# One layer of a hybrid mixer and expert network: state-space jobs brought forward, attention moved back, and the order of their branches exchanged

## The chip, the cores and the metric

The kernel runs on one core of one Trainium2 chip. The metric is the device time of one execution in microseconds (us). TensorE (PE) multiplies matrices; its results land in PSUM, eight banks of 128 x 512 numbers. VectorE (DVE) and ScalarE (ACT) read them from there. GpSimd (POOL) computes from the on-chip memory SBUF, and SyncE (SP) issues the transfers. Each engine executes its own list of instructions strictly in order, and the lists are tied together by semaphores only.

## What is computed

512 latent tokens and 256 context tokens of width 1024 go through one layer: a modulated norm, one input projection, four mixers side by side, a gated sum of the four, an output projection, and a mixture of 32 experts.

```python
q, k, v, z, xbc, dtr, fu, su = _split_in(h @ w_in)
att = _window_attention(q, k, v, kc, vc, sink)           # 8 heads, window 128, plus all context keys
y, _, _ = _ssm_bidir(xs, bm, cm, dt, a_log, fin_f, fin_b, True)
ssm = _ssm_out(y, xs, z, d_skip, ssm_norm_w)             # state-space mixer, both directions, chunks of 128
branches = jnp.stack([att, ssm, _fourier(fu), _short_conv(su, sconv_w)], axis=2)
gates = jax.nn.sigmoid(h @ w_gate + b_gate).reshape(b, l, N_BRANCHES, d)
proj = jnp.einsum("blnw,nwd->blnd", branches, w_branch)
out = jnp.sum(gates * proj, axis=2) @ w_o
```

Branch 0 is attention, 1 the state-space mixer, 2 the Fourier mixer, 3 the short convolution.

## The kernel before

`timeline()` (line 63) writes out one list of steps, and every engine walks through the same list and emits its part of each step. So the order of that list is the order on every engine. The stretch that matters is the merge. For each branch n in `MIX_ORDER` and each of 8 column tiles d it has ("gate", n, d), 24 matmuls whose result ScalarE turns into `gth` (a tanh), and ("proj", n, d), 4 matmuls of the branch (the branch tile); VectorE multiplies the two and, from the second branch on, adds the product into `merged`. Before each gate ScalarE and VectorE split a weight tile into a high and a low part (`ring_hi`, `ring_lo`).

Behind every gate and every proj stand two calls of `side()` (line 114), the points. A point may put in one step of attention or one state job:

- `attention()`: step h puts in, for even h, O(h/2-2), T(h-2) and S(h/2), and for odd h only T(h-2). S(p) computes the scores of a pair of heads p into banks 3 and 4, with four or five blocks of 128 keys; a fifth block goes to bank 2 for the first head and bank 6 for the second (job "S5"). VectorE scales, masks and takes the maximum of each head, ScalarE takes the exp (`sc`), VectorE normalises (at the T job with the odd number before it), T transposes the probabilities on TensorE into banks 5 and 6, ScalarE copies them (`PT`), O multiplies by the values into bank 2. 16 pairs, the middle eight (4 to 11) with five blocks.
- state jobs: `st` (10 of them, each after an `xdd` that GpSimd makes only when the st before it is done), then for each of 4 chunks and 2 groups G, seg, seg, yoff, y; then ynorm, three empty places and four ytr. G goes to `Gm` on VectorE; seg multiplies `Am` from GpSimd and ScalarE takes its exp into `E`, which VectorE multiplies by `Gm`; yoff and y are read by VectorE into `ytmp`.

`bank_plan()` (line 180) gives each step its bank. `claim` (line 501) makes TensorE wait, ahead of a step's first matmul, until the step that had the bank before has been read. All state jobs but ytr are on bank 7, except that G, y and one seg of chunks 2 and 3 are on banks 3 and 5. A T with an odd number also waits until the next pair's S5 is read:

```python
        elif k in ("G", "y") and s[1] >= 2:
            b = 3
        elif k == "seg" and s[1] >= 2 and s[3]:
            b = 5
```

```python
                if h % 2 and ("S5", (h + 1) // 2) in plan:
                    job_read(pe, ("S5", (h + 1) // 2))
```

The order of branches is 3, 2, 0, 1. Attention stands at every odd point from the first on and a state job at every even one, so that attention ends with the second branch, and the state jobs of chunks 2 and 3 run in the third. After the merge come the output projection ("wo"), whose input `mhi`, `mlo` is written in the last branch, the reload of x into `H` (issued when the last proj is done), the routing, and a loop over the experts, whose weights stream from HBM. GpSimd zeroes `xr` behind the last product of the merge (line 1827) and scatters it to the rows that are never used.

Of the kernel before, what the change touches and what calls it, by code (L numbers as in the profile page):

```python
# [19 lines left out]
FR = mybir.dt.float32r  # L20
# [6 lines left out]
P = 128  # L27
D, KD = 1024, 8
S, NCH = 512, 4
# [4 lines left out]
NE, NG, EPG = 32, 8, 4  # L34
# [22 lines left out]
R_DTB, R_ALOG, R_D, R_SINK, R_RB, R_IE, R_IG, R_IB, R_IH = 0, 16, 32, 40, 48, 80, 112, 120, 248  # L57
R_N = 376

MIX_ORDER = (3, 2, 0, 1)  # L60


def timeline():

    t = [("mr", 0), ("mr", 1), ("ssq",), ("mr", 2), ("ssqc",), ("mr", 3), ("mod", 0)]
    t += [("v",), ("vc",), ("dt",)]
    macc = 0

    def tile(*jobs):


        nonlocal t, macc
        t += [*jobs, ("macc", macc)]
        if macc > 4 and macc % 4 == 1:
            t += [("mod", macc // 4)]
        macc += 1

    for m in range(6):
        tile(("xbc", m), ("xbcc", m))
    tile(("k",), ("kc",))  # L80
    for m in range(4):
        tile(("fu", m), *([("rot", 0)] if m == 0 else []))
    t += [("dec",)]
    for m in range(4):
        tile(("q", m), *([("rot", m)] if m else []))
    for m in range(4):
        tile(("cg", m), *([("rot", 4)] if m == 0 else []))
        tile(("sx", m))
        tile(("bg", m))
    for i in range(4):  # L90
        tile(("zk", i))
    t += [("macc", 31)] + [("z", c) for c in range(NCH)]
    t += [("xtr", c) for c in (4, 5, 0, 1, 2, 3)] + [("btr", 0), ("btr", 1), ("mod", 8)]

    att_step = 0

    def attention():

        nonlocal att_step
        h, att_step = att_step, att_step + 1  # L100
        even = h % 2 == 0
        return ([("O", h // 2 - 2)] * (even and h >= 4) + [("T", h - 2)] * (2 <= h < 34) + [("S", h // 2)] * (even and h < 32))

    t += [("V", 0), ("V", 1), ("F", 0)] + attention() + [("V", 2), ("F", 1)] + attention()
    t += [("V", 3), ("F", 2)] + attention() + [("F", 3)] + attention()

    ssm = [("st", d, k) for k in range(5) for d in range(2)]
    for c in range(NCH):
        for g in range(2):
            ssm += [("G", c, g), ("seg", c, g, 0), ("seg", c, g, 1), ("yoff", c, g), ("y", c, g)]  # L110
    ssm += [("ynorm",)] + [None] * 3 + [("ytr", c) for c in range(NCH)]
    point = 0

    def side():

        nonlocal point
        point += 1
        if point % 2 == 1 and att_step < 35:
            return attention()
        if ssm and (point % 2 == 0 or point % 4 == 3 or len(ssm) < 5):  # L120
            return [x for x in [ssm.pop(0)] if x]
        return []

    for i, n in enumerate(MIX_ORDER):
        if i == 3:
            t += [x for x in ssm if x]
            ssm = []
        for d in range(8):
            t += [("gate", n, d)] + side() + side() + [("proj", n, d)] + side() + side()
    for d in range(8):  # L130
        t += [("wo", d)] + ([("sw",)] if d == 1 else []) + ([("rtk", d - 2)] if d > 1 else [])
    t += [("rtk", 6), ("ssq2",), ("rtk", 7), ("rt",)] + [("h2tr", c) for c in range(NCH)] + [("cnt",), ("bexp",), ("tab",)]
    return t
# [20 lines left out]
def tile_order():  # L154

    steps, order, first, last = timeline(), [], {}, {}
    for i, s in enumerate(steps):
        x = tile_of(s)
        if x is not None:
            if x not in last:  # L160
                order.append(x)
                first[x] = i
            last[x] = s


    cut = [x for x in order if is_split(x)]
    need = dict(first)
    for i, x in enumerate(cut):
        need[x] = first[cut[i - 2]] - 0.5 if i > 1 else 0
    soonest = len(steps)  # L170
    for x in reversed(order):
        if x[0] != "macc":
            soonest = need[x] = min(need[x], soonest)
    return sorted(order, key=lambda x: need[x]), last
# [5 lines left out]
def bank_plan(steps):  # L180


    used, plan, rot = {}, {}, 0
    for s in steps:
        k = s[0]
        if k in ROT3:
            b = rot % 3
            rot += 1
        elif k in ("gate", "proj", "O"):
            b = ("gate", "proj", "O").index(k)  # L190
        elif k == "S":
            b = 3
        elif k == "sw":
            b = 5
        elif k == "h2tr":
            b = 3 + s[1] % 2 * 2
        elif k in ("V", "T"):
            b = 5
        elif k in ("xtr", "btr", "F", "ytr"):
            b = 3 + s[1] % 2 * 4  # L200
        elif k in ("G", "y") and s[1] >= 2:
            b = 3
        elif k == "seg" and s[1] >= 2 and s[3]:
            b = 5
        elif k == "ssq2" or s == ("mod", 0):
            b = 0
        elif k == "ssqc":
            b = 1
        elif k == "ssq":
            b = 3  # L210
        elif k in ("ynorm", "macc", "zk", "rtk", "dt"):
            continue
        elif k == "mr":
            b = 4 + s[1]
        elif k == "z":
            b = 3 + s[1]
        elif k == "rt":
            b = 7
        elif k == "cnt":
            b = 2  # L220
        elif k == "tab":
            b = 2
        else:
            b = 7
        used[b] = used.get(b, 0) + 1
        plan[s] = (b, used[b])
        if k == "S" and len(head(2 * s[1])[3]) > 4:
            used[2] = used.get(2, 0) + 1
            plan["S5", s[1]] = (2, used[2])
    return plan  # L230


def head(h):


    blk, g, j = h // 8, h % 2, h // 2 % 4
    if blk == 0:
        return blk, g, j, [0, 1, 4, 5], 3 * P
    keys = [4, 5] + [c for c in (blk - 1, blk, blk + 1) if c < NCH]
    return blk, g, j, keys, 0  # L240
# [33 lines left out]
def build(nc, xT, ctxT, adaw, stream, consts, cossin, dft, cols, rows, wv, wrt, umap, wa, wb, w2, h2d, ybuf, outT):  # L274
# [3 lines left out]
    def at(name, off, shape, dt=F32):  # L278
        return nc.alloc_sbuf_tensor_at(name, shape, dt, offset=BASE + off)
# [11 lines left out]
    hcx = at("hcx", 157888, [P, KD, SC])  # L291
    hchi = at("hchi", 118976, [P, KD, SC], FR)
    hclo = at("hclo", 49152, [P, KD, SC], FR)
    mhi = at("mhi", 110784, [P, KD, S], FR)
    mlo = at("mlo", 49152, [P, KD, S], FR)
    dftm = at("dftm", 49152, [P, 2, NCH, S])
    merged = at("merged", 49152, [P, KD, S])
# [19 lines left out]
    qT = at("qT", 127168, [P, 4, S])  # L317
    dts = at("dts", 127168, [P, 8, 96])
    WV = at("WV", 130240, [P, KD, VD])
    ssmT = at("ssmT", 127168, [P, 4, S])  # L320
    kT = at("kT", 135360, [P, S])
    kcT = at("kcT", 137408, [P, SC])
    vt = at("vt", 138432, [P, 6, P])
# [10 lines left out]
    def up(n):  # L334
        return (n + 31) // 32 * 32
# [25 lines left out]
    m0 = SLOTS * 3 * UNIT * 4  # L361
# [1 line left out]
    um = at("um", m0, [P, UM_N]); m0 += up(UM_N * 4)  # L363
    ru = at("ru", m0, [P, 2]); m0 += 32
    vrow = at("vrow", m0, [P, 2, NTAB]); m0 += up(2 * NTAB * 4)
    swk = at("swk", m0, [P, KD, NE]); g16 = at("g16", m0, [P, 4, NCH, 16]); m0 += 1024
    swv = at("swv", m0, [P, NE]); m0 += 128
    rst = at("rst", m0, [P, 2, NCH]); m0 += 32
    lg = at("lg", m0, [P, NCH, NE]); m0 += 512
    both = at("both", m0, [P, 2, NCH, NE]); sel = at("sel", m0, [P, NCH, NE]); m0 += 512  # L370
# [36 lines left out]
    def bk(b, n=1):  # L407

        return psum[:, b:b + n, :].rearrange("p b n -> p (b n)")

    steps = timeline()
    plan = bank_plan(steps)
    full = [ctx.enter_context(nc.semaphore(f"bank_full{i}")) for i in range(8)]
    empty = [ctx.enter_context(nc.semaphore(f"bank_read{i}")) for i in range(8)]

    def sem(name):
        return ctx.enter_context(nc.semaphore(name))
# [18 lines left out]
    gate_done, merge_done = sem("gate_done"), sem("merge_done")  # L436
# [55 lines left out]
    def job_full(eng, s):  # L492
        b, n = plan[s]
        eng.wait_ge(full[b], n)

    def job_read(eng, s):

        b, n = plan[s]
        eng.wait_ge(empty[b], n)
# [17 lines left out]
    def _(sp):  # L517
# [11 lines left out]
        for i, x in enumerate(order):  # L529
# [12 lines left out]
            if x == ("wo", 2):  # L542

                job_full(sp, ("gate", MIX_ORDER[-1], 7))
                job_full(sp, ("proj", MIX_ORDER[-1], 7))
                sp.dma_start(WR[:, :, :], wrt).then_inc(wr_in, 16)
# [469 lines left out]
    def _(act):  # L1016
        t = Tally(act)
        def A(out, in_, f, **kw):
            return nc.scalar.activation(out, in_, f, **kw)  # L1019
# [20 lines left out]
        for s in steps:  # L1040
# [142 lines left out]
            elif k0 == "gate":  # L1183
                n, d = s[1:]
                b, _n = plan[s]
                job_full(act, s)
                i = MIX_ORDER.index(n) * 8 + d
                if i:

                    job_read(act, ("proj", MIX_ORDER[(i - 1) // 8], (i - 1) % 8))  # L1190
                else:
                    job_read(act, ("z", 3))
                    act.wait_ge(half_ready, 1)
                A(gth[:, :], bk(b), ACT.Tanh, scale=0.5, bias=half[:, n * 8 + d:n * 8 + d + 1]).then_inc(*t(empty[b], plan[s][1]))
            elif k0 == "proj" and s[1] == MIX_ORDER[-1]:

# [590 lines left out]
    def _(g_):  # L1787
        t = Tally(g_)
        G_ = nc.gpsimd

        def hb(ap, n):
            return ap.unsqueeze(2).to_broadcast([P, ap.shape[1], n])

        seg_i = 0
        for s in steps:
            k0 = s[0]
            t.settle()
            if k0 == "st":
                d, k = s[1:]
# [10 lines left out]
            elif k0 == "seg":  # L1810
# [10 lines left out]
                if g == 0:  # L1821
                    if c:
# [1 line left out]
                    G_.tensor_tensor(xd[:, d, :].rearrange("p (h n) -> p h n", h=8),  # L1824
                                     xs[:, c, :].rearrange("p (h n) -> p h n", h=8),
                                     hb(dtv[:, c, d * 8:d * 8 + 8], HD), ALU.mult).then_inc(*t(xd_ready))
        g_.wait_ge(merge_done, 32)
        for h in range(2):
            G_.memset(xr[h][:, :], 0.0).then_inc(*t(xr_zero))
        t.settle()  # L1830
# [196 lines left out]
```

## Time and profile before

| | |
|---|---|
| median of three runs | 1328.28 us (1327.74 to 1329.34) |
| the profiled execution | 1328.5 us |
| its span, first to last instruction | 1326.7 us |
| TensorE busy | 1183.2 us, 89% |
| VectorE busy | 520.0 us, 39% |
| ScalarE busy | 303.5 us, 23% |
| GpSimd busy | 127.2 us, 10% |
| mean DMA rate over the span | 207 GB/s |

The span divides by what goes on: norms and modulation to some 50 us, the input projection to some 285, transposes and the Fourier mixer to 336, the merge with its attention steps and state jobs to 738, the output projection to some 798, the routing to some 831, the experts to some 1280, the final norm to the end. In a timeline row the first number is the start within the span and the second the length; a matmul's end is modelled, so the start of the next instruction is the better mark of how long TensorE needs. In brackets stands the idle time of the engine ahead of the row and what ended it. "L600", "L1286" and "L1019" are lines of helpers, so that operations are told apart by their tiles.

### The profile page before, as it was taken

Reading aid. Unit: us, or ns where it says so; the run is one execution under the profiler, and the core shown is the slowest. Engines: PE = TensorE matmul, PEld = TensorE weight load, DVE = VectorE, ACT = ScalarE, POOL = GpSimd, SP = SyncE. Lnnn points to the kernel's source line nnn. Section 1 sums busy time; section 2 is a strip of 40 time slices with the busy share of each in tenths; the row PEclk is TensorE's granted clock in tenths of the full one; section 3 lists DMA queues with packets and bytes.
Section 4 is the critical chain, followed back from the end, with each engine's and each line's share of the span. In section 5 each row is a group of like instructions: output and inputs, shape, how many; then the busy total and the mean of one; then the engine's idle time right before and its main releaser. Section 6 shows DMA issues by size and latency. Waiting matters only on the chain.

```text
span 1326.7 us, 15684 instructions
## 1 busy us (share of the span) xinstructions
PE 1183.2 (89%) x5560; PEld 699.7 (53%) x5560; DVE 520.0 (39%) x914; ACT 303.5 (23%) x514; POOL 127.2 (10%) x182
## 2 busy tenths in 40 slices
PE   6799999989999999999999895599999997777844
PEld 1588878864666666666666684233333332222212
DVE  2776457632576676544433336011110100001016
ACT  2633122231333334212322233011111110000002
POOL 0000000000111010111000100122121121111110
PEclk9899799989999999999999896799999999999987
DMA  9234535430011111112122301999999999999942
GB/s 390 80 131 149 197 127 214 170 109 0 30 67 65 48 49 48 49 48 82 62 96 95 136 16 71 405 408 423 425 418 420 429 417 425 427 425 426 425 171 105
DMA packets 40019, 274.50 MB, mean 207 GB/s; under 512 B 7428, under 2 KB 7940, under 8 KB 28064
## 3 DMA queue, kind: packets, MB, share of 16 engines
q1 hardware_dynamic: 34208, 265.41, 49.7%
q0 software_dynamic: 5760, 8.41, 1.7%
q8 instruction: 32, 0.52, 0.2%
q14 instruction: 19, 0.16, 0.0%
HBM read 270.90 MB, written 13.37 MB: 214 GB/s over the span
## 4 chain that ended last, share of the span: by engine, by line
PE 73%; DMA 15%; DVE 7%; ACT 2%; issue 1%; SPq 0%; DVEq 0%; ACTq 0%; POOLq 0%; POOL 0%
PE psum L600 70%; DMA ering<-in_wb 11%; DMA Hx<-in_xT 1%; PE psum L824 1%; PE psum L929 1%; DVE amx L1499 1%; DMA gat<-expert_rows 1%; DVE sc L1488 1%; DMA xr<-token_rows,tabt 1%; DMA H<-in_xT 1%; PE psum L949 1%; PE psum L1007 0%; DVE ytmp L1286 0%; ACT E L1019 0%; ACT Hx L1019 0%
## 5 line engine op out<-in xcount | busy, mean ns | idle before, releaser
L600 PE MATMUL psum<-ering,xs 128*64 128x512 f32 x1056 | 242.1, 608 | 41.0 <-DMA ering<-in_wb 22.4
L600 PE MATMUL psum<-Hhi,ring_hi 128*128 128x512 f32 x472 | 195.9, 415 | 1.0 <-ACT gth L1019 1.0
L600 PE MATMUL psum<-Hlo,ring_hi 128*128 128x512 f32 x472 | 186.7, 396 | 0.0
L600 PE MATMUL psum<-Hhi,ring_lo 128*128 128x512 f32 x472 | 185.4, 393 | 0.0
L1286 DVE TENSOR_TENSOR sg<-sg,psum 128x256 f32<-128x256 f32 x66 | 27.8, 421 | 380.9 <-ACT sg L1019 379.7
L600 PEld LDWEIGHTS psum<-ering,xs 128*64 128x64 f32 x1056 | 73.3, 139 | 187.2 <-issue 132.8
L600 PE MATMUL psum<-ering,at 128*64 128x512 f32 x528 | 119.5, 597 | 0.8 <-ACT at L1019 0.8
L1286 DVE TENSOR_TENSOR ring_lo<-ring,ring_hi 128x1024 fp32r<-128x1024 f32 x71 | 87.7, 1235 | 51.6 <-ACT ring_hi L1019 50.2
L600 PEld LDWEIGHTS psum<-Hhi,ring_hi 128*128 128x128 f32 x472 | 89.7, 190 | 27.5 <-issue 9.0
L600 PEld LDWEIGHTS psum<-Hlo,ring_hi 128*128 128x128 f32 x472 | 89.8, 190 | 21.8 <-issue 4.3
L600 PEld LDWEIGHTS psum<-Hhi,ring_lo 128*128 128x128 f32 x472 | 89.6, 190 | 20.2
L1019 ACT ACTIVATE ring_hi<-ring 128x1024 fp32r<-128x1024 f32 x71 | 75.3, 1060 | 90.5 <-PE psum L600 49.2
L1019 ACT ACTIVATE sg<-psum 128x256 f32<-128x256 f32 x33 | 12.7, 384 | 277.6 <-PE psum L600 277.6
L600 PEld LDWEIGHTS psum<-ering,at 128*64 128x64 f32 x528 | 35.5, 136 | 65.0 <-issue 65.0
L1807 POOL TENSOR_TENSOR xdd<-xs,wdd 128x512 f32<-128x512 f32 x10 | 10.4, 1043 | 392.4 <-DVE zs L1475 285.6
L1019 ACT ACTIVATE ysb<-psum 128x512 f32<-128x512 f32 x33 | 19.7, 597 | 123.2 <-PE psum L600 118.7
L1019 ACT ACTIVATE gth<-psum,half 128x512 f32<-128x512 f32 x32 | 22.0, 688 | 108.3 <-PE psum L600 108.3
L1837 POOL DMA_INDIRECT xr<-token_rows,idx x35 | 37.0, 1056 | 30.6 <-POOL idx L1843 30.6
L1019 ACT ACTIVATE sc<-sc,amx 128x512 f32<-128x512 f32 (+1 forms) x32 | 24.8, 775 | 60.4 <-DVE amx L1500 60.4
L600 PE MATMUL psum<-ada,sil 128*2 128x512 f32 x64 | 29.3, 616 | 9.5 <-DMA ada<-in_adaw 9.5
L1578 DVE SCALAR_TENSOR_TENSOR mtmp<-gth,psum 128x512 f32<-128x512 f32 x24 | 16.5, 687 | 54.5 <-PE psum L600 51.1
L1850 POOL DMA_INDIRECT expert_rows<-ysb,idx x33 | 34.1, 1035 | 28.5 <-POOL idx L1857 28.5
(300 smaller groups left out, 1501.9 us busy)
## 6 DMA issues: line engine op xcount, KB each, us to landing
ering<-in_wa SPq DMA_DIRECT2D x28, 2048.0 KB, 18.3
ering<-in_wb SPq DMA_DIRECT2D x28, 2048.0 KB, 23.0
ering<-in_w SPq DMA_DIRECT2D x28, 2048.0 KB, 26.5
ring<-in_stream SPq DMA_DIRECT2D x87, 512.0 KB, 4.1
ada_ring<-in_stream SPq DMA_DIRECT2D x32, 512.0 KB, 3.3
ada<-in_adaw SPq DMA_DIRECT2D x4, 2048.0 KB, 17.6
gat<-expert_rows SPq DMA_DIRECT2D x4, 1024.0 KB, 8.2
Hx<-in_xT SPq DMA_DIRECT2D x1, 2048.0 KB, 16.6
```

Of the source, the lines that this page charges most:

```text
L600: return nc.tensor.matmul(out, lhsT, rhs, start=start, stop=stop)
L824: ins = nc.tensor.transpose(bk(b, 2)[:, i * P:i * P + P], sc[:, h % 3, i * P:i * P + P], ID)
L929: ins = nc.tensor.transpose(XT[h][:, q * P:q * P + P], xr[h][:, q * P:q * P + P], ID)
L949: ins = nc.tensor.transpose(AT[h][:, q * P:q * P + P], sg[h][:, q * P:q * P + P], ID)
L1019: return nc.scalar.activation(out, in_, f, **kw)
L1286: return V_.tensor_tensor(out, a, b, op)
L1488: ins = V_.scalar_tensor_tensor(sc[:, h % 3, 0:S], bk(3 + g), HD ** -0.5, CT[:, C_MASK + mo:C_MASK + mo + S], ALU.mult, ALU.add)
L1499: link(V_.tensor_reduce(amx[:, h, 0:1], sc[:, h % 3, 0:W], AX.X, ALU.max))
L1578: V_.scalar_tensor_tensor(merged[:, d, :] if first else mtmp[:, :], gth[:, :], 1.0, bk(b), ALU.add, ALU.mult).then_inc(*t(empty[b], plan[s ...
L1807: G_.tensor_tensor(xdd[:, :].rearrange("p (h n) -> p h n", h=8), xs[:, c, :].rearrange("p (h n) -> p h n", h=8), hb(wdd[:, c, d * 8:d * 8 ...
L1837: G_.indirect_dma_start(out=xr[h][:, :], out_offset=None, in_=token_half, in_offset=bass.IndirectOffsetOnAxis(ap=at_rows, axis=0), bounds_ ...
L1850: G_.indirect_dma_start(out=row_half, in_=rows_[:, :], in_offset=None, out_offset=bass.IndirectOffsetOnAxis(ap=idx[:, 2 + h:3 + h], axis=0 ...
```

## The change

The order of branches becomes 3, 2, 1, 0. A point now takes a state job whenever one is left, and behind it, besides, an attention step: up to point 64 (the first two branches) at every fifth point, after that at two of three. State jobs must be done when the third branch begins, attention when the fourth does. The rule that put jobs of chunks 2 and 3 on banks 3 and 5 is gone. `mhi` and `ssmT` change places in SBUF, `swk` and `swv` too, and GpSimd zeroes `xr` only behind the last tile of the output projection, because `mhi` now overlaps that region.

```diff
-MIX_ORDER = (3, 2, 0, 1)
+MIX_ORDER = (3, 2, 1, 0)
...
         nonlocal point
         point += 1
-        if point % 2 == 1 and att_step < 35:
-            return attention()
-        if ssm and (point % 2 == 0 or point % 4 == 3 or len(ssm) < 5):
-            return [x for x in [ssm.pop(0)] if x]
-        return []
+        out = [ssm.pop(0)] if ssm else []
+        if att_step < 35 and (point % 5 == 1 if point <= 64 else point % 3):
+            out += attention()
+        return [x for x in out if x]
 
     for i, n in enumerate(MIX_ORDER):
-        if i == 3:
+        if i == 2:
             t += [x for x in ssm if x]
             ssm = []
+        if i == 3:
+            while att_step < 35:
+                t += attention()
...
         elif k in ("xtr", "btr", "F", "ytr"):
             b = 3 + s[1] % 2 * 4
-        elif k in ("G", "y") and s[1] >= 2:
-            b = 3
-        elif k == "seg" and s[1] >= 2 and s[3]:
-            b = 5
...
-    mhi = at("mhi", 110784, [P, KD, S], FR)
+    mhi = at("mhi", 149696, [P, KD, S], FR)
...
-    ssmT = at("ssmT", 127168, [P, 4, S])
+    ssmT = at("ssmT", 157888, [P, 4, S])
...
-    swk = at("swk", m0, [P, KD, NE]); g16 = at("g16", m0, [P, 4, NCH, 16]); m0 += 1024
-    swv = at("swv", m0, [P, NE]); m0 += 128
+    swk = at("swk", 98304, [P, KD, NE]); g16 = at("g16", m0, [P, 4, NCH, 16]); m0 += 1024
+    swv = at("swv", 99328, [P, NE])
...
-        g_.wait_ge(merge_done, 32)
+        job_full(g_, ("wo", KD - 1))
```

How this moves TensorE's instructions is seen at two places. The first, before the change, is TensorE's list from the last score matmuls of S(9) to G(0,1), around the last branch tile of the first branch. `kT` and `kcT` belong to S, `xd,E` is y(0,0), `scT` the branch tile, `CT,sc` T(17), `xbcT` alone G.

```order
L600 MATMUL psum<-kT,qT 128x128 [waits bank_read5,bank_read2]
L600 MATMUL psum<-kT,qT 128x128
L600 MATMUL psum<-xd,E 128x64 [waits xd_ready,m_ready,bank_read7]
L600 MATMUL psum<-xd,E 128x64 x7
L600 MATMUL psum<-scT,ring 128x512 [waits bank_read1]
L600 MATMUL psum<-scT,ring 128x512 x3
L824 MATMUL psum<-CT,sc 128x128 [waits bank_read2,prob_ready,bank_read5]
L824 MATMUL psum<-CT,sc 128x128 x4
L600 MATMUL psum<-xbcT 128x128 [waits bank_read7]
```

The same two state jobs after the change, on TensorE, now around the branch tile of d = 3. `Am,CT` is the second seg of chunk 0, `prevS,xbcT` its yoff.

```order
L598 MATMUL psum<-Am,CT 128x512 [waits am_ready,bank_read7]
L598 MATMUL psum<-prevS,xbcT 128x256 [waits bank_read7] x2
L598 MATMUL psum<-scT,ring 128x512 [waits bank_read1]
L598 MATMUL psum<-scT,ring 128x512 x3
L598 MATMUL psum<-xd,E 128x64 [waits xd_ready,m_ready,bank_read7]
L598 MATMUL psum<-xd,E 128x64 x7
L598 MATMUL psum<-xbcT 128x128 [waits bank_read7]
```

Between y and G, both on bank 7, stood a branch tile and a T job; now G follows y directly, and yoff follows seg.

The second place is S(9) and T(17) on TensorE after the change, which now stand behind the first branch tile of the third branch.

```order
L822 MATMUL psum<-CT,sc 128x128 [waits prob_ready,bank_read5]
L822 MATMUL psum<-CT,sc 128x128 x4
L598 MATMUL psum<-kcT,qT 128x128 [waits bank_read3]
L598 MATMUL psum<-kcT,qT 128x128 x3
L598 MATMUL psum<-kT,qT 128x128 x4
L598 MATMUL psum<-kT,qT 128x128 [waits bank_read5,bank_read2]
L598 MATMUL psum<-kT,qT 128x128
L822 MATMUL psum<-CT,sc 128x128 [waits bank_read2,prob_ready,bank_read5]
L822 MATMUL psum<-CT,sc 128x128 x4
L598 MATMUL psum<-Hhi,ring_hi 128x512 [waits bank_read0,lo_ready,hi_ready]
```

The wait for bank_read2 at T(17) is the one for S5 of pair 9. In the first fence y(0,0) and the branch tile stood between it and S(9); now nothing does. The same holds for S(11) and T(21).

## Rows read from the trace of the kernel before

**Rows 1.** The page: its head and TensorE's busy time.

```profile
span 1326.7 us, 15684 instructions
...
PE 1183.2 (89%) x5560; PEld 699.7 (53%) x5560; DVE 520.0 (39%) x914; ACT 303.5 (23%) x514; POOL 127.2 (10%) x182
```

**Rows 2.** Table by stretches: window: length, then PE, PEld, DVE, ACT, POOL, PEclk, DMA.

```profile
330.00:552.00 222.00, 217.46 (x1278) 148.94 (x1276) 146.82 (x306) 82.39 (x158) 23.66 (x22) 1.00 0.15 53
552.00:740.00 188.00, 185.34 (x717) 124.57 (x716) 79.63 (x115) 45.28 (x61) 12.40 (x11) 0.99 0.19 68
748.00:757.00 9.00, 6.25 (x29) 5.34 (x28) 3.01 (x4) 4.60 (x6) 0.00 (x0) 0.78 0.44 168
```

**Rows 3.** TensorE's waits by releaser, 330 to 740 us (total, times, longest).

```profile
PE psum L600 <- ACT E L1019: 2.4, 4, 0.9
PE psum L600 <- DVE prevS L1286: 1.8, 3, 1.0
```

**Rows 4.** Timeline at an st job and the gate behind it (start, length, engine).

```profile
362.83 0.65 PE L600 MATMUL psum<-xdd,btm 128*64 128x256 f32 x4
...
363.41 0.50 PE L600 MATMUL psum<-Hhi,ring_hi 128*128 128x512 f32 x1
...
363.62 1.05 POOL L1807 TENSOR_TENSOR xdd<-xs,wdd 128x512 f32<-128x512 f32 x1 [3.61 <-PE psum L600]
...
369.11 1.09 PE L600 MATMUL psum<-PT,vt 128*64 128x128 f32 x16
```

**Rows 5.** Timeline at a yoff job, a branch tile and a y job.

```profile
639.92 1.13 PE L600 MATMUL psum<-prevS,xbcT 64*128 64x256 f32 x4
...
640.98 3.70 PE L600 MATMUL psum<-attT,ring 128*128 128x512 f32 x8
641.15 0.69 DVE L1286 TENSOR_TENSOR ytmp<-psum,dec 128x512 f32<-128x512 f32 x1 [3.58 <-PE psum L600]
644.51 1.89 PE L600 MATMUL psum<-xd,E 128*128 128x64 f32 x16
```

**Rows 6.** Timeline from an S step to the second seg behind it.

```profile
461.84 0.71 PE L600 MATMUL psum<-kcT,qT 64*128 64x128 f32 x8
...
463.26 1.12 PE L600 MATMUL psum<-Am,CT 128*128 128x512 f32 x2
...
464.23 3.60 PE L600 MATMUL psum<-uT,ring 128*128 128x512 f32 x8
...
465.98 0.29 DVE L1495 SCALAR_TENSOR_TENSOR sc<-psum,CT 128x128 f32<-128x128 f32 x1
...
469.26 1.12 PE L600 MATMUL psum<-Am,CT 128*128 128x512 f32 x2 [0.89 <-ACT E L1019]
...
470.47 0.60 ACT L1019 ACTIVATE E<-psum 128x512 f32<-128x512 f32 x1 [0.53 <-PE psum L600]
```

**Rows 7.** Timeline at y(2,0) and the G(2,1) behind it.

```profile
580.43 1.89 PE L600 MATMUL psum<-xd,E 128*128 128x64 f32 x16
...
583.51 0.42 DVE L1286 TENSOR_TENSOR ytmp<-ytmp,psum 128x256 f32<-128x256 f32 x1
...
583.98 0.48 PE L600 MATMUL psum<-xbcT 64*128 64x128 f32 x2 [1.66 <-DVE ytmp L1286]
```

**Rows 8.** Timeline from an S step with four key blocks to yoff.

```profile
507.15 0.71 PE L600 MATMUL psum<-kcT,qT 64*128 64x128 f32 x8
...
508.25 1.13 PE L600 MATMUL psum<-Am,CT 128*128 128x512 f32 x2
...
513.55 1.13 PE L600 MATMUL psum<-prevS,xbcT 64*128 64x256 f32 x4 [0.31 <-ACT E L1019]
```

**Rows 9.** Timeline of GpSimd and of VectorE around the output projection.

```profile
740.34 0.99 POOL L1829 MEMSET xr<- 128x512 f32 x2 [122.41 <-DVE merged L1286]
...
796.93 0.75 DVE L1603 SCALAR_TENSOR_TENSOR H<-psum,A,H 128x512 f32<-128x512 f32 x1 [4.24 <-PE psum L600]
...
831.23 1.03 POOL L1837 DMA_INDIRECT xr<-token_rows,tabt  x1 [84.78 <-DVE tabt L1731]
```

## The prediction

> **What bounds the kernel now.** I first read the page's busy table and the chain that ended last: TensorE is busy for 1183.2 us of a 1326.7 us span [rows 1], and its matmuls make most of the chain. Then the table by stretches. In the part that the change reorders, 330 to 740 us, TensorE is busy 217.46 of 222 us and 185.34 of 188 us [rows 2]: 7.20 us of idle in 410. So the reader should see two things. Nothing but TensorE's own work bounds this part, and since the change removes no matmul, it can win 7.2 us there at most. What it can lose is open: each new wait of TensorE, which executes strictly in the order of the list, goes onto the end. The waits by releaser [rows 3] say what the 7.2 us are: an E tile (exp) still being read on ScalarE, a state result still being read on VectorE; and single waits, the longest of them 1.66 us, which comes up below.
>
> Behind 740 us the work is serial (output projection, routing, experts) and nothing there runs ahead of the last branch, so a shift at 740 us reaches the end one to one.
>
> **The change, part by part.** The matmuls are the same before and after; I price only waits. Prices are start-to-start times of a job and the next one allowed on the same bank, minus the time TensorE needs for the job itself. A gate takes 5.7 us on TensorE (363.41 to 369.11 [rows 4]), a branch tile 3.53 us (640.98 to 644.51 [rows 5]).
>
> Before, one state job stands at a point and then a gate or a branch tile, which hides the reading of bank 7. After, two state jobs follow each other behind every gate and every branch tile. Jobs 1 to 10 are st, then per chunk G, seg, seg, yoff, y twice, so the 58 jobs make 29 pairs. All are on bank 7, because the rule that gave banks 3 and 5 to chunks 2 and 3 is gone too.
>
> *Pairs of st.* Five, one with attention between its halves; four are bare. The second st needs xdd, which GpSimd makes only after the first st: start 362.83, GpSimd 363.62 plus 1.05, so 1.9 us with the handoff, while the st itself takes 0.58 [rows 4]. 4 x 1.4 = 5.5 us.
>
> *Pairs inside a chunk.* Of 20, four (G, seg) have attention between and cost nothing in themselves; 16 are bare:
> - seg, yoff and seg, seg: ScalarE starts the exp 1.21 us after the seg starts and takes 0.60 [rows 6]; next job at 1.86, seg itself 0.97 (463.26 to the branch tile at 464.23). 8 x 0.89 = 7.1 us.
> - yoff, y: VectorE starts reading at 1.23 and takes 0.69 [rows 5], next job at 1.98, own time 1.06: 3 x 0.92. The fourth stands behind a branch tile of branch 2, where VectorE first does the product and the addition of that tile and is late by 0.44: 1.36. Together 4.1 us.
> - y, G: the trace has exactly this pair once, behind a branch tile after the first branch: y starts at 580.43, VectorE first multiplies and adds the tile and prepares its sum, reads the bank at 583.51 for 0.42, and G starts at 583.98 after 1.66 us of idle [rows 7]. One pair is like that: 1.66. One is in the first branch, without the addition (0.6 us shorter): 1.05. Two are behind a gate, where VectorE is free and only the 0.42 us read and the handoff stand: 0.75 each. Together 4.2 us.
>
> Sum 15.4 us.
>
> *A seg behind an attention step.* Its exp is queued on ScalarE behind the two softmax exps. In the trace the S step starts at 461.84 and bank 7 is free at 469.26, 7.42 us later [rows 6]. After the change, S (1.42), seg (0.97) and then a gate (5.7) cover it, but for chunks 1 and 3 only a branch tile (3.53) follows: 7.42 - 5.92 = 1.5 us, twice: 3.0 us.
>
> *The third branch.* Two of three points hold an attention step, so T(2p-1) stands directly behind S(p) four times. For pairs 9 and 11, which have a fifth key block, T waits until VectorE has read the second head's fifth block, 466.27 - 461.84 = 4.43 us after S starts [rows 6]; S itself takes 1.42. 2 x 3.06 = 6.1 us. Pair 13 has four blocks and a gate behind it, which covers everything. Pair 15 has four blocks and only a branch tile before the next O, which waits for T's copy behind the exps: 6.4 us after S starts (507.15 to 513.55, where it was an exp of the same 0.60 [rows 8]). S (1.10), T (some 0.5, an estimate: four of the transposes of which five take 0.7) and the tile cover 5.2: 1.2 us. Sum 7.3 us. VectorE was busy 146.82 of 222 us with one pair per gate and the state jobs beside it [rows 2]; a third more pairs without state jobs I take as no bound yet.
>
> *At no cost.* ynorm now stands before an attention step and a gate, which hide its table loads. The zeroing of xr and its scatters move from the end of the merge to behind the last output projection: GpSimd took 740.34 to 746.45 for them and then idled 84.78 us until 831.23; from about 797 (the last H update) it would be done near 804 [rows 9]. If that cover were gone it would cost up to 6.1 us. The new places of mhi, ssmT, swk and swv move no instruction, and no DMA is added: WR, um and H are still issued behind the last branch tile, whichever branch it is.
>
> **Sum.** Added 5.5 + 15.4 + 3.0 + 7.3 = 31.2; removed: at most the old 7.2, and all of it, since each old wait belongs to a pattern that I have priced anew. Net +24.0. Against the profiled execution's own 1328.5 us that is 1352.5; the median of the runs is 0.2 us lower, which I leave.
>
> The ends: no handoff price could be under zero, so a gain is bounded by -7.2 us. Above, the dearest price seen for a pair (1.66) for all 20 bare pairs gives 33 instead of 21, or +36 in all.
>
> **A rule of the Trainium skill.** The trace shows a granted clock of 1.00 and 0.99 over the stretches with the idles of up to 1.66 us, and 0.78 in the 9 us that hold a 2.75 us wait [rows 2]. That is between the two levels of 1.2 and 2.4 GHz; a fall of this kind in the reordered part is rival 4 below. The Trainium skill, "TensorE: Matmul & The Clock Gate", section "A second HAM failure mode: psum-queue depth-cycling", says that a kernel which cycles through PSUM banks and so pauses briefly and often can make the clock swing between its levels. By that rule the sum would be some 10 us worse; the rows of this case show pauses of the size added here without it, only less often.
>
> **The rivals.**
> 1. *Forecast: the pairs cost their turnaround.* For it: the one such pair in the trace cost 1.66 us as computed. 1347 to 1358 us, likeliest 1352.5. Chance 0.68.
> 2. *VectorE was the hidden limit and moving attention away frees it.* The old waits on prevS and ytmp come from VectorE's queue. If TensorE then found bank 7 read each time, the pairs and the third branch cost nothing and the idle goes: 1328.5 - 7.2 = 1321.3 us, faster. It decides from the point where the mean added wait of the 25 places (20 bare pairs, 2 seg, 3 in the third branch) falls under 0.3 us (7.2 / 25). Against it: the reads themselves take 0.42 to 0.69 us plus handoff. Chance 0.03.
> 3. *Half of it is absorbed*, because waits in a row share one cause, so that the job behind a late one finds its input ready: +12, 1340.5 us. Chance 0.12.
> 4. *The clock falls* under the frequent pauses: at a mean granted 0.95, a quarter of the way from 1.00 to the 0.78 of [rows 2], over the some 200 us of the first two branches, 200 x 0.05 = 10 us more: 1362.5 us. Chance 0.08.
> 5. *VectorE becomes the bound in the third branch*, attention steps queueing there: six steps late by 1.5 us, +9: 1361.5 us. Chance 0.06.
> 6. *It cancels*: within 0.2% of before (2.7 us, about what a measurement of this kernel can tell from no change). Chance 0.03.
>
> **How the numbers follow.** The forecast, rival 1, is the likeliest: 1352.5 us. The range 1340 to 1362 takes in 1, nearly all of 3 and parts of 4 and 5. Faster: rival 2, 0.03. Same: 0.03. Slower: the rest, 0.94.
>
> **What would show it.** In the changed profile TensorE's waits between 330 us and the end of the merge should sum to near 31 us instead of 7. By releaser: xdd on GpSimd or prevS four times about 1.4; E on ScalarE ten times, eight near 0.9 and two near 1.5; ytmp on VectorE eight times from 0.7 to 1.7; and in the third branch two waits near 3 us of T for the VectorE read of sc. H's load, near 740 now, should be issued near 764. The expert stage should keep its length. The clock row over the merge should stay at 1.0. Wrong would be: waits for bank 7 missing in the bare pairs (rival 2), a clock row of 0.9 (rival 4), or waits for VectorE in the third branch at places I have not named (rival 5).

## The result, and the profile after

The changed kernel takes 1364.05 us (median of four runs, 1357.71 to 1366.76) against 1328.01 us before: slower, ratio 1.0264 with a 95% interval of 1.0226 to 1.0303. With five more runs of it, taken later, the nine lie between 1357.71 and 1370.06 us with a median of 1364.42. The forecast of 1352.5 us had the sign, the place and the waits; the time is 12 us further up and 2 us outside the range.

The page of the profiled execution, which is the fastest of the nine (1357.71 us), against [rows 1]: the same 5560 matmul instructions keep TensorE busy for 8.3 us more.

```profile
span 1355.9 us, 15684 instructions
...
PE 1191.5 (88%) x5560; PEld 700.6 (52%) x5560; DVE 516.6 (38%) x914; ACT 303.5 (22%) x514; POOL 128.9 (10%) x182
```

TensorE's waits by releaser in the merge of the changed kernel, 342 to 771.2 us (total, times, longest), against [rows 3]:

```profile
PE psum L598 <- ACT E L1017: 9.1, 10, 1.5
PE psum L598 <- DVE ytmp L1284: 7.6, 8, 1.7
PE psum L822 <- DVE sc L1493: 6.2, 2, 3.1
PE psum L598 <- DVE prevS L1284: 4.0, 2, 2.0
PE psum L598 <- POOL xdd L1805: 3.1, 2, 1.6
PE psum L598 <- ACT PT L1017: 1.3, 1, 1.3
PE psum L598 <- DVE attT L1509: 0.8, 1, 0.8
```

They sum to 32.1 us, where 31.2 were forecast and 7.2 stood before. This is ten waits on E, eight on ytmp, four at st pairs, two of 3.1 us in the third branch: the list of the prediction, entry by entry. One is new, 0.8 us on attT.

The start of the merge is the first matmul of the first gate. Its end is marked by SyncE's issue of WR, which waits for the last branch tile. In the kernel before:

```profile
336.14 0.48 PE L600 MATMUL psum<-Hhi,ring_hi 128*128 128x512 f32 x1
...
738.80 0.33 SPq L546 DMA_DIRECT2D WR<-in_wrt  x1
```

In two profiled executions of the changed kernel, the first and one of the later five (1365.19 us):

```profile
333.18 0.47 PE L598 MATMUL psum<-Hhi,ring_hi 128*128 128x512 f32 x1
...
771.17 0.33 SPq L544 DMA_DIRECT2D WR<-in_wrt  x1
```

```profile
337.30 0.47 PE L598 MATMUL psum<-Hhi,ring_hi 128*128 128x512 f32 x1
...
778.60 0.33 SPq L544 DMA_DIRECT2D WR<-in_wrt  x1
```

The merge ends 32.4 us later in one and 39.8 us later in the other. But it also starts at different times, 3.0 us earlier than before in the first and 1.2 us later in the second, although the change leaves the order of the instructions ahead of it as it was. Its own length is 402.7 us before, 438.0 and 441.3 us after: 35.3 and 38.6 us more. The waits account for 32.1 - 7.2 = 24.9 us in both, since the second execution has the same list of waits to the tenth. What is left is 10.4 and 13.7 us, and it is no wait. The table by stretches of the two executions (window: length, then busy time of PE, PEld, DVE, ACT, POOL, and PEclk, the granted clock as a share of 2.4 GHz), first the one of 1357.71 us, then the one of 1365.19 us:

```profile
342.00:556.00 214.00, 189.46 (x872) 123.80 (x871) 110.95 (x214) 52.14 (x90) 37.24 (x32) 0.96 0.13 45
556.00:600.00 44.00, 44.00 (x234) 31.02 (x234) 23.90 (x44) 15.44 (x25) 0.00 (x0) 1.00 0.21 72
600.00:690.00 90.00, 82.53 (x512) 58.72 (x510) 53.20 (x114) 35.91 (x71) 0.00 (x0) 0.96 0.15 53
690.00:771.20 81.20, 81.20 (x302) 54.95 (x299) 27.04 (x35) 19.18 (x25) 0.00 (x0) 1.00 0.22 78
```

```profile
342.00:556.00 214.00, 190.24 (x861) 124.71 (x860) 106.86 (x205) 50.00 (x86) 38.25 (x33) 0.94 0.13 47
...
600.00:690.00 90.00, 82.52 (x529) 58.74 (x528) 56.85 (x123) 35.69 (x71) 0.00 (x0) 0.96 0.15 53
```

In the first execution the clock is below 1.00 exactly in the two stretches that hold the waits, and 1.00 in the two that hold none. The reader should compare [rows 2], where the same work ran at 1.00 and 0.99. What the clock took can be estimated from these rows, as the missing share times the length: 0.04 x 214 + 0.04 x 90 = 12.2 us in the first, 0.06 x 214 + 0.04 x 90 = 16.4 us in the second, 0.01 x 188 = 1.9 us before. The differences, 10.3 and 14.5 us, are close to the 10.4 and 13.7 us that were left. What a lower clock does to a matmul is seen behind the wait of 1.66 us at G(2,1) in the timeline of the changed kernel (start, length, engine):

```profile
482.20 0.49 PE L598 MATMUL psum<-xbcT 64*128 64x128 f32 x2 [1.66 <-DVE ytmp L1284]
...
483.46 0.42 PE L598 MATMUL psum<-Hlo,ring_hi 128*128 128x512 f32 x1
483.69 0.62 PE L598 MATMUL psum<-Hhi,ring_lo 128*128 128x512 f32 x1
484.11 0.63 PE L598 MATMUL psum<-Hhi,ring_hi 128*128 128x512 f32 x1
484.53 0.63 PE L598 MATMUL psum<-Hlo,ring_hi 128*128 128x512 f32 x1
```

From 483.69 on they start 0.42 to 0.43 us apart instead of 0.23: the lower level, 1.2 GHz. Behind the merge the changed kernel gains 3.2 us back in both executions: 1.7 between the issue of WR and that of the first expert weights, the rest behind it. Over the 87 to 89 us of the first of these stretches the clock was 0.85 in both executions and 0.83 before, which would account for the 1.7; the rest stays open.

### The profile page after: what moved, and what is told of

It is laid out like the page before. It is cut to its first block, busy times and chain, and to the rows that moved or that the text cites. A ratio compares the mean times of both kernels' runs of the same rounds, so it can differ in the third digit from the quotient of the medians.

```text
span 1355.9 us, 15684 instructions
## 1 busy us (share of the span) xinstructions
PE 1191.5 (88%) x5560; PEld 700.6 (52%) x5560; DVE 516.6 (38%) x914; ACT 303.5 (22%) x514; POOL 128.9 (10%) x182
## 4 chain that ended last, share of the span: by engine, by line
PE 47%; DMA 17%; DVE 6%; issue 2%; ACT 1%; SPq 0%; POOL 0%; DVEq 0%; ACTq 0%; POOLq 0%
PE psum L598 44%; DMA ering<-in_wb 14%; PE psum L822 1%; PE psum L927 1%; DMA gat<-expert_rows 1%; DMA xr<-token_rows,tabt 1%; DMA xr<-token_rows,idx 1%; DVE sc L1486 1%; DVE ytmp L1284 1%; DVE amx L1497 1%; DMA H<-in_xT 1%; ACT E L1017 0%; PE psum L947 0%; DVE x L1780 0%; PE psum L1005 0%
## 5 line engine op out<-in xcount | busy, mean ns | idle before, releaser
L598 PE MATMUL psum<-ering,xs 128*64 128x512 f32 x1056 | 245.4, 614 | 38.6 <-DMA ering<-in_wb 21.0
L1284 DVE TENSOR_TENSOR sg<-sg,psum 128x256 f32<-128x256 f32 x66 | 27.8, 421 | 381.5 <-ACT sg L1017 380.4
L1017 ACT ACTIVATE PT<-psum 128x512 f32<-128x512 f32 (+1 forms) x32 | 20.8, 651 | 86.6 <-PE psum L822 74.6
L1835 POOL DMA_INDIRECT xr<-token_rows,idx x35 | 36.9, 1055 | 30.6 <-POOL idx L1841 30.6
```

What stands on the lines that cost most here:

```text
L598: return nc.tensor.matmul(out, lhsT, rhs, start=start, stop=stop)
L1284: return V_.tensor_tensor(out, a, b, op)
L1835: G_.indirect_dma_start(out=xr[h][:, :], out_offset=None, in_=token_half, in_offset=bass.IndirectOffsetOnAxis(ap=at_rows, axis=0), bounds_ ...
```

## The experiments

Two theories stood at the start. **A**: the loss is the waits, 25 us, and beside them a falling clock, which costs a different amount in each execution. **B**: the loss is the waits, and the excess over the forecast sits elsewhere and is fixed. Each kernel is the changed one with the edit shown, unless another is named. The first four experiments ran in one session, in which the kernel before had a median of 1327.58 us; the last four in another, where it had 1326.23 us. For one profiled execution of each, the merge from its first matmul to the issue of WR:

| kernel | length, us | waits, us | length less waits | mean clock |
|---|---|---|---|---|
| before | 402.7 | 7.2 | 395.5 | 1.00 |
| changed, first | 438.0 | 32.1 | 405.9 | 0.97 |
| changed, again | 441.3 | 32.1 | 409.2 | 0.97 |
| two banks | 414.0 | 16.4 | 397.6 | 0.99 |
| old bank rule | 427.6 | 27.0 | 400.6 | 0.98 |
| attention spread | 431.3 | 27.8 | 403.5 | 0.98 |
| fillers | 427.9 | 12.9 | 415.0, with added work | 1.00 |
| two banks, two xdd buffers | 405.7 | 10.6 | 395.1 | 0.99 |
| all together | 392.3 | 0 | 392.3 | 1.00 |
| pairs in the kernel before | 459.9 | 44.1 | 415.8 | 0.94 |

Apart from the fillers, all do the same work in the merge. The column without the waits grows as the clock falls, from 392 to 398 us at 0.99 and above to 416 us at 0.94: that is the clock's part of the loss.

**The changed kernel again.** No edit.

> The changed kernel unchanged, to see how it spreads. Theory A (waits and clock): TensorE's waits in the merge are 32 us in every execution, the time varies with the granted clock: 0.952 goes with 1358 us and 0.946 with 1366 us, about 8 us for 0.006, and a profile at a lower mean clock shows it low for more of the merge, with the same waits. Theory B (waits alone, and the excess over 1352.5 us sits in a stretch behind the merge): a slower execution has the merge as long as the 1357.7 us one and the expert stage longer.

Measured: 1364.42 us (1362.30 to 1370.06, five runs), waits 32.1 us, whole-span clock 0.947 against 0.952. The span is 7.4 us longer than in the first profile (1363.3 against 1355.9). Of this 3.3 us arise in the merge, without a wait being longer, and 4.1 us ahead of it, where TensorE was busy for 5.2 us more with the same instructions and the clock from 285 us to the first gate was 0.86 instead of 0.96. Over the nine runs the time by and large rises as the whole-span clock falls, from 0.952 at 1357.71 us to 0.944 at 1370.06. So theory A's claim holds, but less than half of this difference is the merge's. Theory B's longer expert stage is not there.

**Two banks for state jobs.**

```diff
+        elif k in ("st", "G", "seg", "yoff", "y"):
+            b = 7 if used.get("jobs", 0) % 2 else 3
+            used["jobs"] = used.get("jobs", 0) + 1
```

> State jobs alternate between bank 3 and bank 7, so that the two of a pair never share a bank; order of steps untouched. The 16 bank waits inside the chunks (13.7 us in the changed kernel's trace) and most of the two seg waits (3.0 us) go; st keeps a wait of some 1.6 us four times for xdd. Waits in the merge fall from 32 to some 17 us. Theory A: the time falls by 15 us for the waits and by 3 to 8 us more since the clock stays up, to 1341 to 1346 us. Theory B: it falls by 15 us only, to 1349 us, with the clock as in the changed kernel. Rival that VectorE's queue and not the bank is what is waited for: the waits stay, under other names, and the time stays within 4 us.

Measured: 1337.08 us (1333.34 to 1339.91, six runs), ratio to before 1.0067. The waits left in the merge, by releaser (the rows of the output projection, swk and mlo, left out):

```profile
PE psum L825 <- DVE sc L1496: 6.2, 2, 3.1
PE psum L601 <- POOL xdd L1808: 5.8, 4, 1.6
...
PE psum L601 <- DVE attT L1512: 1.8, 1, 1.8
PE psum L601 <- ACT PT L1020: 1.3, 1, 1.3
PE psum L601 <- ACT E L1020: 1.3, 2, 0.7
```

16.4 us instead of 32.1: every wait on ytmp and most on E are gone; the two st waits on prevS are now waits on xdd, 1.6 instead of 2.0 us. So the bank was what TensorE waited for inside the chunks, not VectorE's queue. But the time fell by 27 us, not by 16. The clock over the first two branches, 0.94 and 0.96 in the changed kernel's two profiles, was 0.99. Theory A had the direction and was too low (15 plus 3 to 8): the clock gave back some 11.

**The old bank rule put back.** The four deleted lines return.

> Only the deleted bank rule is put back: G, y and one seg of chunks 2 and 3 on banks 3 and 5. Of the waits in these chunks those of seg before yoff, seg before seg and yoff before y go (some 5.2 us), y before G stays (both on bank 3). Theory A: 5 us and up to 3 us of clock, 1356 to 1359 us. Theory B: 1359 us. If the deleted rule were what costs most, the time would fall by more than 10 us.

Measured: 1353.62 us (1351.22 to 1361.10, four runs). Waits 27.0 us, so 5.1 less, as priced. The time fell by 10.8 us against the 1364.42 of the same session, twice the waits. It is below what both theories gave; theory A's allowance for the clock (3 us) was again too small. A fall of more than 10 us had been named as the sign that the deleted rule costs most. The fall is just that, but the waits do not bear the reading out: the rule brings back 5.1 of the 24.9 us that were added, and two banks for all state jobs bring back 15.7.

**Attention spread in the third branch.**

```diff
-        if att_step < 35 and (point % 5 == 1 if point <= 64 else point % 3):
+        if att_step < 35 and (point % 5 == 1 if point <= 64 else point < 69 or point % 2):
```

> Only the placing of attention in the third branch is altered: one step behind each gate and each branch tile (two behind the first two), with the odd T ahead of an S instead of right behind it. The two waits of 3.08 us for the fifth block and the one of 1.3 us for the copy go: 7.5 us less, and under theory A 1 to 3 us of clock besides: 1353 to 1357 us. Theory B: 1356.5 us. If VectorE were the bound in that branch, as rival 5 had it, the waits would reappear on sc and the time fall by less than 3 us.

Measured: 1355.93 us (1354.33 to 1357.23, four runs). The two waits of 3.1 us and the one of 1.3 us are gone, but two new ones on PT have come (1.1 and 1.9 us), where O stands directly behind a T. So the waits fell by 4.3, not 7.5 us, and the time by 8.5: inside the range that was expected (1353 to 1357 us), though 7.5 us of it had been expected from the waits and only 1 to 3 from the clock. By its time alone this run would not separate the theories. The clock of the third branch, 0.96 in the changed kernel, was 1.00 over everything behind 556 us. VectorE is no bound in that branch.

**Fillers.** The test that separates the clock from the waits: TensorE multiplies constants where it would wait.

```diff
+        jobs = ("st", "G", "seg", "yoff", "y")
+        fill = {}
+        for i_, s in enumerate(steps):
+            if s[0] in jobs and steps[i_ - 1][0] in jobs:
+                fill[s] = (6, 3 if s[0] == "st" else 1)
+            if s in (("T", 17), ("T", 21)):
+                fill[s] = (7, 6)
...
+            if s in fill:
+                fb, fn = fill[s]
+                job_read(pe, last_t if fb == 6 else ("ytr", 3))
+                for _ in range(fn):
+                    mm(bk(fb)[:, 256:512], CT[:, C_ONE:C_ONE + P], CT[:, 0:256], True, True)
```

> The changed kernel with matmuls of constants that nobody reads, put where TensorE waits: three ahead of the second st of a pair, one ahead of every other second state job, six ahead of T(17) and T(21) (28 or more such matmuls, about 0.48 us each, into columns of banks 6 and 7 that no job uses). No real job can start earlier; TensorE only does something while it would wait. Theory A (a good third of the loss is the clock falling after pauses): the sum of TensorE's idle in the merge falls from 32 to some 15 us, the clock of the merge stays near 1.00, and the time falls by 4 to 10 us although work was added: 1354 to 1360 us. Theory B (the clock has no part): the time stays at 1364 us or rises by a few us, since a filler can make a job later.

Measured: 1352.89 us (1351.49 to 1354.88, five runs): 11.5 us below the 1364.42 of the other session, 10.2 us faster when each is taken against the kernel before of its own session. It has 40 matmuls more (80 instructions of the profile) whose results nobody reads. The clock of its first two branches, and the issue of WR:

```profile
342.00:556.00 214.00, 202.60 (x985) 133.50 (x984) 114.28 (x221) 56.53 (x97) 38.27 (x33) 1.00 0.13 47
```

```profile
764.58 0.33 SPq L544 DMA_DIRECT2D WR<-in_wrt  x1
```

TensorE's idle in the merge is 12.9 us, the clock 1.00. The edit only adds waits and work, so it makes nothing ready for a real job sooner than in the changed kernel. Still the merge is 10 and 13 us shorter than in the two executions of that kernel. It is 25.2 us longer than before the change, where the added waits alone would give 24.9. This settles it for theory A. The spread of the executions shrinks from 8 us to 3, too.

**Two xdd buffers** on top of two banks.

```diff
-    xdd = at("xdd", 73728 + 12288, [P, S])
+    xdd = [at("xdd0", 73728 + 12288, [P, S]), at("xdd1", 65536 + 2048, [P, S])]
...
-                    job_full(g_, st_prev[s])
+                    job_full(g_, st_prev[st_prev[s]] if st_index[s] > 1 else ("F", 3))
```

> The kernel with two banks for state jobs, and besides two xdd buffers, so that GpSimd may prepare the next st while one runs. The four waits of 1.6 us for xdd go in part: GpSimd needs 1.05 us per xdd and a pair of st 1.2 us, and the second buffer is ready early. 5 to 6 us less than with two banks alone (1337.1): 1331 to 1332 us. If the st waits were VectorE's and not GpSimd's, they would reappear on prevS and the time fall by less than 2 us.

Measured: 1331.92 us (1327.65 to 1335.05, ten runs). The st waits are gone altogether, 5.8 us, and the time fell by 5.2 (3.8 when each is taken against the kernel before of its own session). The clock of the first two branches was 0.99 already and had next to nothing left to give.

**All together.** Two banks, two xdd buffers, and attention placed so that S has a gate or a branch tile behind it everywhere.

```diff
-    ssm += [("ynorm",)] + [None] * 3 + [("ytr", c) for c in range(NCH)]
+    ssm += [None] * 2 + [("ynorm",)] + [None] * 5 + [("ytr", c) for c in range(NCH)]
...
-        if att_step < 35 and (point % 5 == 1 if point <= 64 else point % 3):
+        if att_step < 35 and (point % 4 == 0 if point <= 64 else point > 66 and point % 2):
```

> Two banks, two xdd buffers, attention behind every branch tile at every other position (always behind the pair, never between its halves) in the first two branches, then one step per position in the third with gate or branch tile between S and T, ynorm one position later. Every wait that was named should go: TensorE's waits in the merge 2 to 6 us, against 7.2 before the change, the clock at 0.99 or 1.00. The time 1322 to 1328 us. That the branch order as such costs something would show as a time over 1330 with waits under 7 us.

Measured: 1318.58 us (1318.01 to 1320.03, five runs), ratio to before 0.9949 with an interval of 0.9935 to 0.9963: faster than the kernel before and the changed one. In the list of waits no row is left in the merge. Its table by stretches:

```profile
340.00:538.00 198.00, 197.91 (x1010) 133.93 (x1009) 125.62 (x233) 59.99 (x107) 36.30 (x32) 1.00 0.14 52
538.00:731.00 193.00, 193.00 (x956) 133.96 (x955) 97.58 (x177) 64.02 (x106) 0.00 (x0) 1.00 0.21 74
```

TensorE has work in 390.91 of 391 us. So the new order of branches costs nothing by itself, and all the 7.2 us that the kernel before lost here could be won. The gain is 7.7 us by the medians. In the two profiled executions the merge is 10.4 us shorter, of which 7.2 are waits and some 1.9 the clock, which was 0.99 over the last 188 us before.

**Pairs in the kernel before.** Order of branches and places of attention as before the change; only the state jobs are paired.

```diff
+        if ssm and point <= 62:
+            return [x for x in [ssm.pop(0), ssm.pop(0)] if x] if point % 4 == 0 else []
         if ssm and (point % 2 == 0 or point % 4 == 3 or len(ssm) < 5):
             return [x for x in [ssm.pop(0)] if x]
```

> The kernel before the change with one thing altered: its state jobs no longer stand one by one at every even point but in pairs at every second even point, on the same banks; order of branches and places of attention as before. 15 pairs fall into the first two branches: five st pairs at 1.4 us and ten others at 1.0 to 1.6 us on one bank, so waits of 7 become 24 to 28 us, and under theory A 3 to 8 us of clock come on top: 1348 to 1356 us. Theory B: 1345 to 1349 us. If the pairing were harmless and the branch order what costs, the time would stay within 4 us of 1328.

Measured: 1387.84 us (1386.66 to 1389.24, four runs), 32 us above what theory A allowed. Its waits:

```profile
PE psum L602 <- DVE prevS L1288: 16.2, 4, 5.5
PE psum L602 <- DVE ytmp L1288: 12.7, 5, 3.1
PE psum L602 <- DVE Gm L1288: 5.8, 2, 2.9
PE psum L602 <- ACT E L1021: 5.1, 4, 1.6
PE psum L602 <- DVE tmpS L1524: 2.9, 1, 2.9
```

With the 1.4 us on ssmT they make 44.1 us, not 24 to 28. The reading of the first job's bank stands in VectorE's list behind the product of the branch tile and the normalising of a pair of heads. A timeline of VectorE at one such st pair, the first st having started on TensorE at 430.19:

```profile
430.90 0.16 DVE L1288 TENSOR_TENSOR amx<-amx 128x1 f32<-128x1 f32 x1
...
431.30 1.08 DVE L1325 TENSOR_SCALAR sc<-sc,amx 128x640 f32<-128x640 f32 x1
432.11 1.17 POOL L1820 TENSOR_TENSOR Am<-CT,dta 128x512 f32<-128x512 f32 x1
432.41 0.88 DVE L1288 TENSOR_TENSOR amx<-amx 128x1 f32<-128x1 f32 x1
...
433.52 1.10 DVE L1325 TENSOR_SCALAR sc<-sc,amx 128x640 f32<-128x640 f32 x1
...
434.65 1.15 DVE L1288 TENSOR_TENSOR ytmp<-prevS,cds 128x256 f32<-128x256 f32 x1
...
436.31 1.12 PE L602 MATMUL psum<-xdd,btm 128*64 128x256 f32 x4 [5.47 <-DVE prevS L1288]
```

The clock was 0.89 over the stretch from 340 to 470 us and 0.93 from 470 to 590. The merge was 57.2 us longer than before, of which waits are 36.9; the other 20 go with the mean clock of 0.94 in the table above. So the pairing costs without the new order of branches too, and more. By the trace it costs more because attention is not thinned in the first two branches; no run thinned attention alone, so that part is a reading of the trace.

## Why the prediction was wrong

- **The bound and the direction: right.** TensorE's own work bounds the merge, and each added wait reached the end. The kernel with no wait left gained the 7.2 us of idle that the prediction named as the most that could be won there, and some 2 us of clock that it had left out. A shift of the merge's end did not reach the end quite one to one: 3.2 us were won back behind it.
- **Pairs of st: 5.5 forecast, 7.1 measured.** Behind a gate 1.57 us for xdd, near the 1.4; behind a branch tile 1.98 for prevS. The sum had only the way over GpSimd. Behind a branch tile the way over VectorE ends later: 0.69 us for the tile's product, 1.21 for ytmp beside GpSimd's xdd, 0.42 for prevS.
- **Pairs inside a chunk: 15.4 forecast, 13.7 measured.** E mostly 0.74 instead of 0.89; yoff before y 0.85 three times and 1.23, for 0.92 and 1.36; y before G 0.96, 0.58, 1.66 and 0.58 for 1.05, 0.75, 1.66 and 0.75.
- **A seg behind attention: 3.0 forecast, 3.0 measured** (1.54 and 1.44).
- **Third branch: 7.3 forecast, 7.5 measured** (3.08 twice, 1.31). The forecast's 3.06 is 0.05 more than its own 4.43 - 1.42. VectorE did not become the bound.
- **The total, 31.2 for 32.1, is closer than its terms.** Pairs of st were 1.6 us too low and pairs inside a chunk 1.7 too high; that these cancel is luck.
- **"At no cost": right but for ynorm.** Its wait holds up VectorE, so that O(5) is read late and S(7) waits 0.8 us. The zeroing of xr began at 827.64 and GpSimd was idle for 28.55 us before it was needed.
- **The step that failed: the sum treated the added waits as the whole loss and put the clock at nothing.** "The rows of this case show pauses of the size added here without it, only less often": I took pauses that came alone (ten in 410 us) for evidence on pauses that come every 9 us (23 between 342 and 556 us). There the clock was 0.96 and 0.94 in the two profiled executions, and the merge took 10.4 and 13.7 us beyond its waits; with fillers in the pauses the clock was 1.00 and this excess was gone. The rule that I quoted beside it, of the Trainium skill, "TensorE: Matmul & The Clock Gate", section "A second HAM failure mode: psum-queue depth-cycling", agrees with these clocks in its main point, frequent short pauses, though here the pauses come from two jobs on one bank. Rival 4 named the mechanism and its time, 1362.5 us, 2 us from the result, and got a chance of 0.08. Its price of 10 us was about right; the chance was not.
- **The range was narrower than its own working.** The dearest price for every pair gave +36 us, which is 1364.5 us from waits alone. The range ended at 1362 and left out even rival 4's 1362.5.
- **H's load** was expected near 764 and came at 772.02 in the first execution; with the clock held up by fillers WR, just ahead of it, is issued at 764.58.

## What to carry to other kernels

Before two short jobs are put back to back, ask whether the second needs what a reader has not yet freed: on one bank the pair costs the whole trip to the reader and back, and two banks in turn took away 15.7 of 32.1 us of waits here. Add up such waits from the start-to-start times of one trace, which held here within 3% in all and within 30% term by term, but count frequent waits dearer than their length: here 24.9 us more of waits made the merge 35 to 39 us longer. Before putting an excess down to a stretch, compare where it starts in both profiles as well as where it ends. If a wait can't be removed, idle matmuls in it may pay, and nothing pays like having no wait.

## What the runs showed of the hardware that I had not expected

- **Frequent short pauses lower TensorE's clock, by a different amount in each execution.** With the same 32.1 us of waits, none above 3.1 us, the clock over the first 214 us was 0.96 in one execution and 0.94 in another, and the merge took 10.4 and 13.7 us beyond its waits. Forty useless matmuls in these pauses made the kernel 10 to 11.5 us faster. With pauses of 2.9 to 5.5 us, one per some 20 us, the mean granted clock was 0.89 over 130 us.
- **Small VectorE instructions stretch beside GpSimd.** An addition of 128x1 took 0.88 instead of 0.16 us, ytmp 1.21 instead of 0.42, the normalising of 128x640 1.08 instead of 0.55 us, while GpSimd multiplied tiles of 128x512. Each of them began after the GpSimd instruction beside it. In the changed kernel, at 355.89 us, ytmp began 0.04 us ahead of xdd: it took 0.42 us, and xdd 1.28 instead of 1.04. The Trainium skill, "SBUF — State Buffer", section "Who interferes with whom", says that a VectorE instruction with two inputs in SBUF contends with a GpSimd instruction that reads SBUF; the addition of 128x1 and ytmp, which have two, agree with it; that sentence does not cover the normalising, which has one. No run here took GpSimd's work away by itself, so this remains a reading of the trace.
